# Moving the later modulation chunks among the attention heads, and giving the expert weights eight ring slots

## The reference, cut to what matters

```
mod = silu(c) @ w_ada + b_ada                  # 1024 x 6144, six vectors of 1024
shift_m, scale_m, gate_m, shift_f, scale_f, gate_f = split(mod)
h = rmsnorm(x, g_pre_mix) * (1 + scale_m) + shift_m
rq, rk, rv, rg, aq, ak, av = split(h @ w_in)
y_ret = silu(rg) * bidirectional_retention(rq, rk, rv)     # 4 heads
y_att = dilated_attention(aq, ak, av)                      # 8 heads of 64
x = x + gate_m * rmsnorm(concat(y_ret, y_att) @ w_out, g_post_mix)
h = rmsnorm(x, g_pre_ffn) * (1 + scale_f) + shift_f
# each of 16 experts takes its 32 best rows: silu(h @ w_gate) * (h @ w_up) @ w_down, width 2048
x = x + gate_f * rmsnorm(moe, g_post_ffn)
for i in range(2):                             # second block
    x = x + 0.5 * swiglu_ffn(rmsnorm(x, ffn1_norm[i]))
    # recurrence and windowed attention with a relative-position bias, gates, output projection
    x = x + 0.5 * swiglu_ffn(rmsnorm(x, ffn2_norm[i]))
    x = x + sigmoid(rmsnorm(x, ple_norm[i]) @ w_ple_gate[i]) * (p[i] @ w_ple[i])
```

## Time and profile before

| | |
|---|---|
| median of 3 runs | 2504.7 us (2504.56 to 2510.8) |
| profiled execution: its own time, span | 2512.7 us, 2510.9 us |
| granted TensorE clock, mean | 0.882 |
| TensorE, VectorE, ScalarE, GpSimd busy | 78%, 37%, 26%, 2% |
| first expert matmul | 261.69 us |
| first matmul of the layers | 1199.96 us |

### The profile page before, as it was taken

The page is one execution under the profiler, slowest core; times in us unless marked ns, Lnnn a source line. Parts: engine busy times, 40 slices in busy tenths (PEclk is TensorE's granted clock), DMA queues, the critical chain, the costliest instruction groups (busy, mean ns, idle before and its releaser), DMA issues.

```text
span 2510.9 us, 33702 instructions
## 1 busy us (share of the span) xinstructions
PE 1969.8 (78%) x12491; PEld 1370.5 (55%) x12491; DVE 926.8 (37%) x1310; ACT 656.9 (26%) x921; POOL 40.4 (2%) x69
## 2 busy tenths in 40 slices
PE   7887765555565665556999987899989998789998
PEld 4554311111111111111899865799879987668996
DVE  1134000000000000000766655566656666466765
ACT  2011000000000000000544543444444444434443
POOL 0000000000000000000000000000000000000000
PEclk8897878877788778777999997899999999889999
DMA  9872799999999999999555531355535554234551
GB/s 345 314 285 85 325 428 427 428 428 427 428 426 428 428 428 427 427 428 402 175 188 197 178 109 61 132 185 182 186 104 199 175 187 151 84 113 140 200 192 59
DMA packets 172854, 659.78 MB, mean 263 GB/s; under 512 B 10003, under 2 KB 106044, under 8 KB 141764
## 3 DMA queue, kind: packets, MB, share of 16 engines
q1 hardware_dynamic: 169740, 652.03, 67.1%
q10 hardware_dynamic: 2376, 3.03, 0.5%
q0 software_dynamic: 624, 3.16, 0.3%
HBM read 655.55 MB, written 2.64 MB: 262 GB/s over the span
## 4 chain that ended last, share of the span: by engine, by line
issue 77%; PE 15%; DVE 3%; DMA 2%; ACT 1%; POOL 1%; POOLq 0%; SPq 0%; ACTq 0%; DVEq 0%; PEldq 0%; PEld 0%
PE PS L1709 11%; DMA ring<-in_w_ada 2%; PE PS L1460 1%; DVE units L198 1%; DVE arena L198 1%; PE PS L1420 1%; PE PS L1469 1%; POOL arena L571 0%; ACT arena L198 0%; DVE hn L198 0%; SPq L433 0%; DMA mod_rows<-wide 0%; ACT units L198 0%; PE PS L1501 0%; POOLq L598 0%
## 5 line engine op out<-in xcount | busy, mean ns | idle before, releaser
L1709 PE MATMUL PS<-hT_split,units 128*128 128x256 f32 x4416 | 553.7, 285 | 9.9 <-DVE hT_split L198 8.1
L1709 PEld LDWEIGHTS PS<-hT_split,units 128*128 128x128 f32 x4416 | 546.7, 193 | 20.3 <-DVE hT_split L198 11.1
L198 DVE TENSOR_TENSOR units<-ring,units 128x1024 fp32r<-128x1024 f32 (+2 forms) x384 | 466.4, 1215 | 236.8 <-ACT units L198 207.2
L198 ACT ACTIVATE units<-ring 128x1024 fp32r<-128x1024 f32 (+2 forms) x384 | 404.2, 1053 | 515.3 <-PE PS L1709 497.0
L198 DVE SCALAR_TENSOR_TENSOR arena<-arena,PS 128x512 f32<-128x512 f32 (+1 forms) x52 | 41.1, 791 | 823.5 <-ACT arena L198 511.9
L1671 PE MATMUL PS<-moe_ring,arena 128*32 128x512 f32 x1280 | 214.1, 808 | 152.9 <-DMA moe_ring<-in_w_gate_e 73.0
L1709 PE MATMUL PS<-units,hT_split 128*128 128x512 f32 (+2 forms) x1344 | 316.6, 397 | 18.1 <-DVE hT_split L198 18.0
L198 ACT ACTIVATE arena<-PS 32x256 f32<-32x256 f32 (+4 forms) x135 | 66.8, 495 | 977.4 <-PE PS L1679 324.8
L1709 PEld LDWEIGHTS PS<-units,hT_split 128*128 128x128 f32 x1344 | 258.8, 196 | 68.1 <-issue 11.0
L1709 PE MATMUL PS<-units,hid_split 128*128 128x512 f32 x1056 | 255.8, 392 | 0.0
L1671 PEld LDWEIGHTS PS<-moe_ring,arena 128*32 128x32 f32 x1280 | 41.7, 131 | 317.4 <-DMA moe_ring<-in_w_gate_e 114.4
(11 more groups left out here) (197 smaller groups left out, 1066.6 us busy)
## 6 DMA issues: line engine op xcount, KB each, us to landing
moe_ring<-in_w_gate_e SPq DMA_DIRECT2D x48, 2048.0 KB, 25.8
ring<-in_w_down_e SPq DMA_DIRECT2D x48, 2048.0 KB, 27.1
ring<-in_ffn_wi SPq DMA_DIRECT2D x88, 1024.0 KB, 5.4
ring<-in_w_up_e SPq DMA_DIRECT2D x32, 2048.0 KB, 26.1
moe_ring<-in_w_up_e SPq DMA_DIRECT2D x32, 2048.0 KB, 26.3
ring<-in_ffn_wo SPq DMA_DIRECT2D x44, 1024.0 KB, 4.9
ring<-in_w_in SPq DMA_DIRECT2D x40, 1024.0 KB, 5.4
ring<-in_w_gate_e SPq DMA_DIRECT2D x16, 2048.0 KB, 26.9
```

Of the source, the lines that this page charges most:

```text
L198: return instruction(*args, **kwargs)
L1709: passes = [mm(out, lhs[i], rhs[j], start=start and i + j == 0, stop=stop and i == 1, **flags) for i, j in ((0, 0), (0, 1), (1, 0))]
```

## The change

The 16 later modulation fills move: two each behind `rqk`'s halves and `rv`'s first half, ten behind `rv`'s second half; the products follow the same order, two behind heads 0 to 3, four behind heads 4 and 5. VectorE's two `ada_row` calls move with them. The experts' places become eight: `wide` is place 6 (its fill waits for `x_mid`), and `hn` with `hT` behind it, seen as one 2 MB tensor `turned_and_rows`, is place 7 (its fill waits for `logits` and `hn_split`). As `wide` now holds expert weights, the bias band is read by SyncE in `layer_constants`, once in each layer, and GpSimd's one read is gone. The layers' first six fills wait for the use of fills 187 to 189 instead of 189 to 191.

```diff
-ADA_AFTER = (4, 4, 3, 3, 2, 0)
+ADA_AFTER = {("rqk", 0): 2, ("rqk", 1): 2, ("rv", 0): 2, ("rv", 1): 10}
...
-BIG = 6
+BIG = 8
...
+            elif m == 6:
+                v = wide.rearrange("p a n -> p (a n)")
+            elif m == 7:
+                v = turned_and_rows
...
-                    sp.wait_ge(S["big_used"], BIG + MOE_SLOTS - 2 + (pos - POS_LAYER) // 2)
+                    sp.wait_ge(S["big_used"], BIG + MOE_SLOTS - 4 + (pos - POS_LAYER) // 2)
...
-            for (name, col), n in zip(IN_PIECES, ADA_AFTER):
+            for name, col in IN_PIECES:
                 for half in range(2):
-                    fill(POS_IN[name] + half, w_in[:, 4 * half:4 * half + 4, col:col + 512])
+                    fill(POS_IN[name, half], w_in[:, 4 * half:4 * half + 4, col:col + 512])
+                    for _ in range(ADA_AFTER.get((name, half), 0)):
+                        ada_fill(i)
+                        i += 1
                 small_fills(name)
...
-                if 3 <= i < BIG:
+                if 3 <= i < 6:
                     sp.wait_ge(S["slot_used"], POS_LAYER - R + 2 * (i - 3) + 2)
+                elif i == 6:
+                    sp.wait_ge(S["x_mid"], 1)
+                elif i == 7:
+                    sp.wait_ge(S["logits"], 1)
+                    sp.wait_ge(S["hn_split"], 1)
...
                 def layer_constants():
+                    sp.wait_ge(S["skew_written"], 16)
+                    sp.dma_start(band, bass.AP(skew.tensor, P, [[3 * P - 1, P], [3 * P * P, SW_H], [1, TOK]])).then_inc(
+                        S["band_full"], 16)
...
-            pool.wait_ge(S["skew_written"], 16)
-            nc.gpsimd.dma_start(band, bass.AP(skew.tensor, P, [[3 * P - 1, P], [3 * P * P, SW_H], [1, TOK]])).then_inc(
-                S["band_full"], 16)
...
             ret_weight(0)
             ret_weight(1)
-            ada_row(2, b_late[:, 1, :])
             att_scores(7)
             ret_weight(2)
             ret_weight(3)
+            ada_row(2, b_late[:, 1, :])
...
-                        dve.wait_ge(S["band_full"], 16)
+                        dve.wait_ge(S["band_full"], 16 * (l + 1))
...
                 if h == 0:
                     in_columns("rqk", 0, 0)
+                    ada_products(8, 2)
                 elif h == 1:
                     in_columns("rqk", 0, 1)
                     piece_end()
-                    ada_products(19, 3)
+                    ada_products(10, 2)
...
                 elif h == 5:
...
+                    ada_products(20, 4)
```

More of the change, by code:

```diff
@@ L50 @@
 IN_PIECES = [("ak", 2048), ("aq", 1536), ("av", 2560), ("rqk", 0), ("rv", 512), ("rg", 1024)]
-ADA_AFTER = (4, 4, 3, 3, 2, 0)
+ADA_AFTER = {("rqk", 0): 2, ("rqk", 1): 2, ("rv", 0): 2, ("rv", 1): 10}
 POS_IN, POS_ADA, _pos = {}, list(range(KT)), KT
[L53 to L56, removed]
+for _name, _ in IN_PIECES:
+    for _half in range(2):
+        POS_IN[_name, _half] = _pos
+        _pos += 1
+        POS_ADA += range(_pos, _pos + ADA_AFTER.get((_name, _half), 0))
+        _pos += ADA_AFTER.get((_name, _half), 0)
 assert len(POS_ADA) == ADA_SLOTS
@@ L229, in build @@
         x = sb("x", [P, NT, D])
+        hn_at = nc.sbuf_base
         hn = sb("hn", [P, NT, D])
+        assert nc.sbuf_base == hn_at + 4 * NT * D
         hT = sb("hT", [P, KT, TOK])
+        turned_and_rows = nc.alloc_sbuf_tensor_at("turned_and_rows", [P, BIG_SLOT], F32, offset=hn_at)[:, :]
         zeros = sb("zeros", [P, TOK])
@@ L466, in _ @@
             i = KT
-            for (name, col), n in zip(IN_PIECES, ADA_AFTER):
+            for name, col in IN_PIECES:
                 for half in range(2):
-                    fill(POS_IN[name] + half, w_in[:, 4 * half:4 * half + 4, col:col + 512])
+                    fill(POS_IN[name, half], w_in[:, 4 * half:4 * half + 4, col:col + 512])
+                    for _ in range(ADA_AFTER.get((name, half), 0)):
+                        ada_fill(i)
+                        i += 1
                 small_fills(name)
-                for i in range(i, i + n):
-                    ada_fill(i)
-                i += n > 0
             for i in range(4):
@@ L980, in _ @@
                 dve.wait_ge(S["piece_done"], done)
-                if done == 3:
-                    dve.wait_ge(S["late_full"], 112)
-                    ada_row(1, b_late[:, 0, :])
                 dve.run(V.tensor_copy, dst.rearrange("p a n -> p (a n)"),
@@ L1007, in _ @@
             att_scores(5)
+            dve.wait_ge(S["late_full"], 112)
             dve.wait_ge(S["piece_done"], 5)
@@ L1010, in _ @@
                     PS[:, 0:2, :].rearrange("p b n -> p (b n)")).then_inc(S["in_copied"], 1)
+            ada_row(1, b_late[:, 0, :])
             att_scores(6)
@@ L1451, in in_half @@
             def in_half(name, half):
-                full(POS_IN[name] + half)
-                return [(k, slot(POS_IN[name] + half, 4, 512)[:, k % 4, :]) for k in range(4 * half, 4 * half + 4)]
+                full(POS_IN[name, half])
+                return [(k, slot(POS_IN[name, half], 4, 512)[:, k % 4, :]) for k in range(4 * half, 4 * half + 4)]
             def in_columns(name, bank, half):
@@ L1486, in _ @@
             mm(PS[0:SW_H, 6, 0:3 * P], relb[:, :], bucket[0:BUCKETS + 1, :], start=True, stop=True).then_inc(S["rep"], 1)
-            ada_products(8, 4)
             for half in range(2):
@@ L1490, in _ @@
             piece_end()
-            ada_products(12, 4)
             for half in range(2):
@@ L1533, in _ @@
             att_s(1)
-            ada_products(16, 3)
             pe.wait_ge(S["in_copied"], 2)
@@ L1550, in _ @@
                     in_rows("rv", 0, 0)
+                    ada_products(12, 2)
                 elif h == 3:
@@ L1553, in _ @@
                     piece_end()
+                    ada_products(14, 2)
                 elif h == 4:
-                    ada_products(22, 2)
                     pe.wait_ge(S["in_copied"], 3)
@@ L1558, in _ @@
                     ret_s(1)
+                    ada_products(16, 4)
                 elif h == 5:
```

## The result

The changed kernel takes 2495.66 us (median of 6 runs, 2490.57 to 2497.12), the kernel before on the same chip 2506.72 us (6 runs, 2504.56 to 2511.7). Paired by rounds the ratio is 0.994, 95% interval [0.9926, 0.9954]: about 15 us faster (11.5 to 18.5 by the interval), where 15.5 were forecast. The two medians taken by themselves differ by 11.1 us only. In a later comparison the same pair gave 2493.69 against 2508.44 us, 0.994 again [0.9921, 0.996], and there the medians differ by 14.8 us. The absolute time is 6.5 us above the forecast 2489.2, which was worked out from 2504.7 us for the kernel before; the median of that kernel itself moves between 2504.7 and 2512.0 us from one comparison to the next.

A forecast was written before the change was run, and what follows sets the result against it. Experts were taken as bound by a full DMA stream, layers by TensorE, the prologue by neither. Places -9.9, order -5.6 and band 0 gave -15.5 us, from 2504.7 to 2489.2 us, own range 2485 to 2493, whole range 2482 to 2499.

The forecast's parts named there:

- The places: Expert stream: two more 2 MB fills move into idle time before the first expert matmul, 2 x 4.93 = 9.9 us less.
- the two places change nothing: Rival, expert stage: it ends by something else or the places fill too late; only -5.6, 2499.1 us; chance 0.08.
- The order: Prologue: modulation products moved among the heads remove TensorE's waits; first expert matmul at 256.1 us, -5.6 us.
- 6.4 us earlier transpose: Behind the heads: the transpose after the retention's root moves from 181.75 to 175.4 us.
- the chain that the forecast put at the end: End of the heads: third modulation row, GpSimd's broadcast, retention's root, then transpose at 175.4 us, with TensorE idling 4 us.
- Up to head 0: Prologue: `av` ends at 80.6 us, first transpose at 85.6 after 3.6 us idle, slow clock costing 2.4 us.
- 1.5 us of waiting for the last products: Head 5: allowance for late weights of modulation products 22 and 23, bounds 0 and 4 us; retention's output at 151.1 us.
- GpSimd's chain: Behind the heads: from the third row's end to the root's pow end 20.4 us, ending at 170.8 us.
- forecast idle time of 4 us: Behind the heads: TensorE idles 4 us for GpSimd's root, where it idled 1.2 us before.
- GpSimd's drain: Retention's root: the drain between add and pow waits for GpSimd's own broadcast to land, read from a 5.16 us gap.
- The first rival: End of the heads: GpSimd's drain does not hold the root, TensorE sets the end; -20.0 us, 2484.7 us; chance 0.16.
- The band: Layers: one 1 MB band read in each, ahead of the last feed-forward gate weights, costs 0 us, bounds 0 to 7.

The follow-up runs named there:

- e2: Kernel before with only the new order of the modulation, six places, band read by GpSimd: 2505.12 us, ratio to before 0.9971.
- e3: Changed kernel, but its two new places filled only after the first and second expert fills are used: 2506.81 us, ratio to before 0.9975.
- e1: Kernel before with only the eight places and the band read in the layers, old modulation order: ratio to before 0.9945, repeated 0.9958.
- e6: Changed kernel with the band read four times in each layer, one read after the other: 2520.57 us in a single run.
- e4: Changed kernel with four modulation products ahead of head 0's transpose and 2, 2, 3, 2, 2, 1 behind heads 0 to 5: 2495.86 us, ratio to before 0.9933.
- e5: e4 with GpSimd's retention root ahead of the third row's write and broadcast: 2490.18 us, again 2491.2; ratios to before 0.9927 and 0.9922.
- e7: e5 with the three gain vectors read behind the `rg` weights instead of ahead of the `rqk` weights: 2485.72 us, ratio to before 0.99.

## Why the prediction was right, step by step

**The places, -9.9 us: right.** The four profiled executions with six places filled ahead of the first expert matmul (before twice, e2, e3) take 922.4 to 923.9 us from it to the last product, the nine with eight 912.0 to 913.1: by the means 10.5 us, against the 9.9 that the prediction held to be all that two fills can take. e3 shows that 9.6 us of it is the early filling; where the rest comes from is open. The rival "the two places change nothing" is out, and it had rested on something else ending the stage.

**The order, -5.6 us: right in size, by misses that cancelled, which is luck.** The mean of the first expert matmul over four profiled executions with the old order (before twice, e1 twice) is 258.5 us, over five with the new (changed twice, e2, e3, e6 with 255.44) 254.1: 4.4 us. By the runs it is 4.1 us (e1 again less changed again) and about 7 us (e2). The forecast had measured its 6.4 us earlier transpose from one trace of the kernel before, at 181.75 us; over the same nine executions the transpose moves from 178.7 to 174.3 us, 4.4 us. And in this execution the chain that the forecast put at the end was not the one that ended last. In its steps:
- Up to head 0, exact: `av` ended at 80.6 us (forecast 80.6), the first transpose stood at 85.71 (85.6) behind 3.69 us of idle time (3.6). The low clock behind that wait cost 2.8 us on transpose, scores and the first half of `rqk` (forecast 2.4).
- The heads ended late. The sum gave TensorE 1.5 us of waiting for the last products, and 3.21 came; and behind this wait the clock fell to half, which the sum had left out at this place. The window of TensorE at the retention's output, columns of the earlier trace rows:

```profile
153.00:155.00 2.00, 2.00 (x12) 2.00 (x11) 0.06 (x1) 0.60 (x1) 0.57 (x1) 0.50 1.06 393
```

  So the retention's output began at 154.67 instead of 151.1 us, and TensorE was through at 175.2 us. In the repeat of the changed kernel the same wait was 1.95 us, and the output ran at full clock:

```profile
149.46 1.07 PE L1433 MATMUL PS<-ring,arena 128*32 128x512 f32 x8 [1.95 <-DMA ring<-in_w_ada]
...
152.12 3.79 PE L1582 MATMUL PS<-arena 128*128 128x128 f32 x32
```

  Of the five executions with this order, three waited 3.21 to 3.98 us here and went on at half clock, two waited 1.95 and 2.58 us (e2) and kept the full one.
- GpSimd's chain was shorter than in the earlier trace rows. GpSimd's timeline, changed kernel:

```profile
159.22 0.56 POOL L601 DMA_DIRECT2D arena<-mod_rows  x1 [5.30 <-DMA mod_rows<-wide]
164.78 0.20 POOL L586 TENSOR_TENSOR head_ms<-head_ms,eps_group 128x8 f32<-128x8 f32 x1 [5.00 <-DVE head_ms L200]
167.81 1.67 POOL L588 TENSOR_TENSOR head_ms<-head_ms,halves 128x8 f32<-128x8 f32 x1 [2.83 <-issue]
```

  And its read-back among the issues of DMAs (count, KB, us to landing):

```profile
arena<-mod_rows POOLq DMA_DIRECT2D x1, 1024.0 KB, 8.3
```

  The broadcast landed in 8.3 us, where 11.4 had been carried over from before, and the pow ended at 169.5 us (forecast 170.8) although the row came 2.7 us late. From the row's end to the pow's end it took 16.4 us, where the sum had 20.4: this is its mis-sized term. The transpose was forecast for 175.4 us and ran at 175.49, but TensorE itself was the last to be ready, by about 1 us. So the forecast idle time of 4 us did not come. In e3 and e6 it was TensorE too; in the repeat of the changed kernel and in e2 TensorE waited for VectorE, 0.47 and 0.51 us: the two chains end together, and which of them decides changes from run to run.

**GpSimd's drain: shown.** The prediction read from one gap of 5.16 us that the drain between add and pow lasts until GpSimd's own transfer has landed. In the changed kernel the pow starts 0.3 us after the landing (167.5), in e4 0.3 us after it (165.4), with gaps of 2.83 and 8.39 us, and with the root ahead of the transfer the gap is 0.33. The first rival (the drain does not hold the root, 20.0 us in all) fails by these rows and by its time, which lies outside the interval of the ratio (11.5 to 18.5 us). That TensorE sets the end, as this rival had it, did come true in three of the five executions, but because TensorE itself was late.

**The band, 0 us: right.** The layers take 1307.8 to 1311.0 us in eight profiled executions that read it there once and 1310.3 to 1310.9 in three that do not (e3, which reads it too, at 1313.9, stands 3 us off, and why is open). The slack behind the 0 is real and larger than read, some 9.6 us for 6.3, and e6 spent it.

**The sum.** -15.5 was forecast, and 0.994 of about 2507 us is -15.0. Of the 6.5 us by which the absolute time missed, 2.0 come from its starting point, the median of 3 runs (2504.7 for 2506.72 us). The other 4.4 are the distance from the forecast 15.5 to the 11.1 us between the two medians of that comparison; in the later one it was 14.8. How much of this is scatter and how much a term that was too large, the runs do not tell.

**What stays open.** The prologue's times scatter with the same instructions: the first expert matmul of the old order lies at 261.7, 261.7, 254.3 and 256.5 us. TensorE's waits for weights up to `av` alone are 6.1, 11.1, 6.1 and 8.3 us there, and `rqk` ran at half clock behind them in the first and at full clock in the others. What decides how late a weight lands there was not settled, so the order's gain is known only to some microseconds. The two executions at 261.7 us are those of the kernel before and the two lower ones those of e1, so an effect of the places on the prologue is not ruled out. Against it: the two at 261.7 got there differently, with `av` beginning at 80.11 and at 86.66 us, and e1's runs gain 10.5 to 13.8 us, which the 11 us of its later stage nearly use up.

## What to carry to other kernels

In a stage that is a pure stream of weights, as this one, each place that is filled before the first use is worth about one fill's time, once; the deeper ring itself gave 1 us at most. When a change removes several waits from one engine, follow the other engines' chains to the same meeting point before counting them: here GpSimd's ended within about 1 us of TensorE's in the changed kernel, and 4.39 us behind it in e4. Where GpSimd both computes and issues transfers, put the computation that others wait for ahead of the transfer. And where the prologue scatters by 7 us from one profiled execution to the next, do not price an edit of 5 us there by one trace of each kernel.

## What the runs showed of the hardware

- A drain on GpSimd lasted until the transfer that GpSimd had issued before it had landed: gaps of 2.83 (changed), 4.50 (e2), 5.16 (before) and 8.39 us (e4) between the same two short instructions, each ending 0.3 to 0.4 us after the landing; 0.33 us with no transfer under way (e5, e7).
- A short wait cost more than its own length. In e5 again TensorE waited 3.75 us for `rqk`, and the windows behind it (columns of the earlier trace rows) show the clock falling to half:

```profile
89.00:91.00 2.00, 0.00 (x0) 0.00 (x0) 0.69 (x1) 1.20 (x4) 0.00 (x0) 1.00 1.07 395
91.00:93.00 2.00, 1.82 (x5) 1.53 (x6) 0.00 (x0) 0.00 (x0) 0.00 (x0) 0.62 1.04 423
93.00:95.00 2.00, 2.00 (x6) 1.56 (x6) 0.00 (x0) 0.00 (x0) 0.00 (x0) 0.52 1.00 423
```

  In e7, behind 1.40 us of waiting at the same place, the clock stayed at 1.00, and the 32 matmuls took 7.17 us instead of 8.86.
- The same 1 MB broadcast through GpSimd's queue took 8.2 to 8.4 us to land in the changed kernel, its repeat, e2 and e3, 9.8 in e6, 11.4 and 11.5 in the kernel before and e4, and 5.3 in e5 again, where it went out last of all, at 167 us. A duration that is carried from one place among the transfers to another needs bounds of this size.
